# Early expert products as three products of rounded parts, and the key picks laid out by place

## The reference

```
q  = (t @ w_q).reshape(n_tok, 8, 2, 128)               # 256 tokens, 1024 -> 2048
sc = einsum("thpd,hpnd->thpn", q, subkeys)             # scores of 128 keys, two halves
sv, si = top_k(sc, 16)                                 # 16 best keys of each half
cand = sv[:, :, 0, :, None] + sv[:, :, 1, None, :]     # 16 x 16 sums
cidx = si[:, :, 0, :, None] * 128 + si[:, :, 1, None, :]
top_v, pos = top_k(cand, 16)
idx = take_along_axis(cidx, pos);  g = softmax(top_v)  # 8 x 16 = 128 experts of 16384 a token
h = einsum("cd,ced->ce", x, u_tab[idx])
out = einsum("ce,ced->cd", g * gelu(h), v_tab[idx])
```

## Time and profile before

| | |
|---|---|
| median of 3 runs | 2599.25 us (2597.35 to 2600.2) |
| profiled execution, its own time | 2601.88 us |
| its span in the profile | 2600.1 us |
| granted TensorE clock, mean | 0.99 |
| busy share TensorE (matmuls), VectorE, ScalarE, GpSimd | 97%, 76%, 50%, 29% |
| HBM read | 420.11 MB, 163 GB/s over the span |
| share of the chain that ended last: TensorE, VectorE, ScalarE | 84%, 8%, 3% |
| first expert layer, its early products and batches | 824.0 to 1007.0 us |

### The profile page before, as it was taken

How to read it: one execution, slowest core, us unless ns; L and a number is a source line. 1 busy time by engine, 2 the same in 40 slices (tenths; PEclk the granted TensorE clock), 3 DMA queues, 4 the chain that set the end, 5 groups by cost and what they waited for, 6 DMA issues and landing times.

```text
span 2600.1 us, 44298 instructions
## 1 busy us (share of the span) xinstructions
PE 2517.9 (97%) x14328; PEld 2216.0 (85%) x14328; DVE 1973.4 (76%) x3589; ACT 1288.8 (50%) x1917; POOL 745.1 (29%) x754
## 2 busy tenths in 40 slices
PE   8799998999999999999999999899999999999998
PEld 6689877998889898888888888789898888888887
DVE  6868768786678998577777777679997577777776
ACT  4756557664552265444444444662265444444443
POOL 0400003000000101255555555320101255555554
PEclk9999999999999999999999999999999999999999
...
DMA packets 170081, 424.66 MB, mean 163 GB/s; under 512 B 13517, under 2 KB 66125, under 8 KB 169214
## 3 DMA queue, kind: packets, MB, share of 16 engines
...
...
HBM read 420.11 MB, written 3.18 MB: 163 GB/s over the span
## 4 chain that ended last, share of the span: by engine, by line
PE 84%; DVE 8%; ACT 3%; issue 3%; DMA 1%; DVEq 1%; POOL 1%; ACTq 0%; POOLq 0%; SPq 0%
PE PS L467 16%; PE PS L468 16%; PE PS L469 16%; PE PS L753 13%; PE PS L842 7%; PE PS L755 7%; DVE oh L2278 2%; PE PS L868 2%; PE PS L481 2%; PE PS L482 2%; PE PS L486 2%; DVE oh L2275 1%; DVE lo L1560 1%; PE PS L662 1%; PE PS L810 1%
## 5 line engine op out<-in xcount | busy, mean ns | idle before, releaser
L1560 DVE TENSOR_TENSOR lo<-raw,hi 128x1024 fp32r<-128x1024 f32 x716 | 1060.3, 1507 | 477.6 <-ACT hi L1010 476.3
L1010 ACT ACTIVATE hi<-raw 128x1024 fp32r<-128x1024 f32 x716 | 747.2, 1052 | 298.8 <-PE PS L469 232.3
L467 PE MATMUL PS<-hi,Ah 128*128 128x512 f32 x1024 | 402.0, 393 | 5.1 <-POOL Al L2445 2.6
L468 PE MATMUL PS<-lo,Ah 128*128 128x512 f32 x1024 | 401.1, 392 | 0.0
L469 PE MATMUL PS<-hi,Al 128*128 128x512 f32 x1024 | 398.9, 390 | 0.0
L753 PE MATMUL PS<-xx,hi 128*128 128x512 f32 x1504 | 371.6, 390 | 0.0
L753 PEld LDWEIGHTS PS<-xx,hi 128*128 128x128 f32 x1504 | 282.5, 188 | 58.4
L1465 ACT ACTIVATE gl<-gl 128x256 f32<-128x256 f32 x188 | 78.5, 417 | 479.8 <-DVE gl L2321 479.8
L2445 POOL TENSOR_TENSOR Al<-kept,Ah 128x256 fp32r<-128x256 f32 x188 | 299.8, 1595 | 14.8
L467 PE MATMUL PS<-xx,hi 128*128 128x256 f32 x992 | 281.6, 284 | 0.0
L469 PE MATMUL PS<-xx,lo 128*128 128x256 f32 x992 | 281.3, 284 | 0.0
...
## 6 DMA issues: line engine op xcount, KB each, us to landing
raw<-in_peer_u SPq DMA_DIRECT2D x256, 512.0 KB, 3.6
raw<-in_peer_v SPq DMA_DIRECT2D x256, 512.0 KB, 4.4
...
```

The costliest lines, as they stand in the source:

```text
L467: pe.matmul(o, ah, bh, start=start, stop=False)
L468: pe.matmul(o, ah, bl, start=False, stop=False)
L1010: cp.activation(hi[:, s, 0:size], raw[:, s, 0:size], ACT.Copy).then_inc(hi_made, 1)
L1560: V.tensor_tensor(lo[:, s, 0:size], raw[:, s, 0:size], hi[:, s, 0:size].bitcast(F32), ALU.subtract).then_inc(lo_made, 1)
```

## The change

In the expert layers, with the names of the diff:

- **More early products, most of them in three parts.** LEAD is 38, 24 of them ahead of the transposes. The first THREE = 25 are computed as `hi` by `xh`, `hi` by `xl` and `lo` by `xh`, in order: 16 matmuls, a wait for the low part, 8 matmuls. The high part is ScalarE's (`u_high`, into four places of the arena, `lead_his`), the low part GpSimd's (`u_low`, into `lo`). SyncE waits for `u_low` instead of `split_used` before it loads such a slot again. The last 13 stay in full precision, so the four additions of `xw` come after product 24 of the three-part kind.
- **Order on GpSimd.** 20 `u_low`, the picks, 5 `u_low`, the additions of `xw`.
- **Picks by place.** The table's outermost axis is m, so a pick writes 256 neighbouring columns. The reduction over m becomes four additions of halves (2048, 1024, 512 and 256 columns a partition). VectorE's part of the weights moves between the two halves' picks. GpSimd's compares get a second operation, times 1.0.
- **Batches.** VectorE first copies first keys and every fourth second key into `firsts`, five to a batch, and compares five groups of 128 in one instruction; three scaled compares follow. The fourth token's one-hot is scaled by its weight on ScalarE (`scaled_to`, two batches ahead). TensorE's operands move accordingly. VectorE waits before batch HOTS - 1 until product THREE - 1 has been computed.
- **First values.** VectorE weighs 16 rows in groups of four, where it did so with 12; ScalarE's first four splits of v wait for h0 + 4p + 8. GpSimd's first two `lead_low` wait for four weighed rows.
- **Places.** Four early rows lie in `spare` (over the places of `Ah` and `Al`), the next 16 in `early`.
- **Attention.** GpSimd's doubling and its addition get a second operation with a constant (plus 0.0; times 1.0 first).

```diff
@@ -98,9 +98,11 @@
-LEAD = 34
-LEAD_FIRST = 20
-LEAD_AFTER = (-1, 3, 8, 14, 19, 24, 30, 35, 40, 46, 51, 57, 63, 63)
+LEAD = 38
+LEAD_FIRST = 24
+THREE = LEAD_FIRST + 1
+LEAD_AFTER = (-1, 6, 11, 15, 20, 25, 30, 35, 40, 46, 51, 57, 63, 63)
+PICK_AT = 20
@@ -152,6 +154,8 @@
+    lead_lows = {plan[f"peer{l}"][0] + j: THREE * l + j + 1 for l in range(2) for j in range(THREE)}
@@ -192,6 +196,7 @@
+        spare = sb("spare", [P, 4, T], F32, offset=here[0])
@@ -201,10 +206,11 @@
-        kept = sb("kept", [P, KEPT - IN_X - 16, T])
+        kept = sb("kept", [P, KEPT - IN_X - 20, T])
...
+        lead_his = [sb(f"lead_hi{n}", [P, 2, BLK], F32R, offset=arena_at + 4 * word) for n, word in enumerate((12288, 29184))]
@@ -226,20 +232,31 @@
+        firsts = con[:, C_MASK:C_MASK + 5 * T // 4].rearrange("p (b t) -> p b t", t=5)
         def bank(n):
...
         def lead_row(layer, j):
-            if j < 16:
-                s = (plan[f"peer{layer}"][0] + LEAD + j // 4) % RING
+            if j < 4:
+                return spare[:, j, :]
+            if j < 20:
+                s = (plan[f"peer{layer}"][0] + LEAD + j // 4 - 1) % RING
...
-                return kept[:, j - 16, :]
+                return kept[:, j - 20, :]
...
+        def lead_hi(j):
+            return lead_his[j % 4 // 2][:, j % 2, :]
+        def lead_lo(j):
+            return lo[:, (j + RING - THREE) % RING, :]
@@ -394,7 +411,7 @@
-        seltmp = [view(8192, TT * PH, TOPK, TOPK), view(4096, TT * PH, TOPK, TOPK)]
+        seltmp = [view(8192, TOPK, TT * PH, TOPK), view(4096, TOPK, TT * PH, TOPK)]
@@ -825,7 +842,10 @@
-                    pe.wait_ge(raw_in[s], landed[n])
+                    if j < THREE:
+                        pe.wait_ge(S("u_high"), THREE * layer + j + 1)
+                    else:
+                        pe.wait_ge(raw_in[s], landed[n])
@@ -836,8 +856,19 @@
+                    if j < THREE:
+                        for k in range(KD):
+                            w = lead_hi(j)[:, k * P:(k + 1) * P]
+                            pe.matmul(PS[:, bk, 0:T], w, xh[:, k, :], start=k == 0, stop=False)
+                            pe.matmul(PS[:, bk, 0:T], w, xl[:, k, :], start=False, stop=False)
+                        pe.wait_ge(S("u_low"), THREE * layer + j + 1)
+                        for k in range(KD):
+                            m = pe.matmul(PS[:, bk, 0:T], lead_lo(j)[:, k * P:(k + 1) * P], xh[:, k, :],
+                                          start=False, stop=k == KD - 1)
+                        m.then_inc(split_used, 1)
+                        return
...
-                        if j == 0 and k % 2 == 0:
+                        if j == THREE and k % 2 == 0:
@@ -863,10 +894,13 @@
-                    pe.wait_ge(S("hot_made"), 5 * (64 * layer + b + 1))
+                    pe.wait_ge(S("hot_made"), 4 * (64 * layer + b + 1))
...
-                        i = pe.matmul(PS[:, bk, k * P:(k + 1) * P], oh[:, b % HOTS, 0, k * P:(k + 1) * P],
-                                      oh[:, b % HOTS, 1, k * P:(k + 1) * P], start=True, stop=True)
+                        if k == 3:
+                            pe.wait_ge(S("hot_scaled"), 64 * layer + b + 1)
+                        x = (k + 1) % 4 * P
+                        i = pe.matmul(PS[:, bk, k * P:(k + 1) * P], oh[:, b % HOTS, 1, x:x + P],
+                                      oh[:, b % HOTS, 0, k * P:(k + 1) * P], start=True, stop=True)
@@ -1414,7 +1448,19 @@
+                def u_high(j):
+                    n = u_block(layer, j)
+                    act.wait_ge(raw_in[n % RING], landed[n])
+                    if j >= 4:
+                        act.wait_ge(split_used, u_block(layer, j - 4) + 1)
+                    cp.activation(lead_hi(j), raw[:, n % RING, :], ACT.Copy).then_inc(S("u_high"), 1)
+                u_high(0)
...
+                for j in range(1, 4):
+                    u_high(j)
@@ -1424,16 +1470,20 @@
-                for j in range(10):
-                    lead(j)
+                def leads_to(first, end):
+                    for j in range(first, end):
+                        lead(j)
+                        if j + 4 < THREE:
+                            u_high(j + 4)
+                leads_to(0, 14)
...
-                for j in range(10, LEAD_FIRST - 2):
-                    lead(j)
+                leads_to(14, LEAD_FIRST - 3)
...
-                for j in range(LEAD_FIRST - 2, LEAD_FIRST):
-                    lead(j)
+                leads_to(LEAD_FIRST - 3, LEAD_FIRST)
@@ -1443,12 +1493,25 @@
+                at = [0]
+                def scaled_to(n):
+                    while at[0] < min(n, 64):
+                        b = at[0]
+                        act.wait_ge(S("hot_made"), 4 * (64 * layer + b) + 1)
+                        o = oh[:, b % HOTS, 1, 0:P]
+                        cp.activation(o, o, ACT.Copy, scale=selT[:, 2, 4 * b + 3:4 * b + 4]).then_inc(S("hot_scaled"), 1)
+                        at[0] += 1
...
+                        scaled_to(b + 2)
...
+                            scaled_to(b + 4)
@@ -1475,7 +1538,7 @@
-                    act.wait_ge(S("lead_weighed"), h0 + 4 * p + 4)
+                    act.wait_ge(S("lead_weighed"), h0 + 4 * p + 8)
@@ -2238,16 +2301,20 @@
-                    last([V.scalar_tensor_tensor(seltmp[c][:, :, :, m], rows, float(m), keys[:, :, m:m + 1].to_broadcast([P, TT * PH, TOPK]),
+                    st = seltmp[c]
+                    last([V.scalar_tensor_tensor(st[:, m], rows, float(m), keys[:, :, m:m + 1].to_broadcast([P, TT * PH, TOPK]),
...
-                    V.tensor_reduce(sel[:, c].rearrange("p t k -> p (t k)"), seltmp[c].rearrange("p g k m -> p (g k) m"),
-                                    AX.X, ALU.add).then_inc(S("sel_made"), 1)
+                    for n in (8, 4, 2):
+                        link(V.tensor_tensor(st[:, 0:n], st[:, 0:n], st[:, n:2 * n], ALU.add))
+                    V.tensor_tensor(sel[:, c].rearrange("p t k -> p (t k)"), st[:, 0].rearrange("p g k -> p (g k)"),
+                                    st[:, 1].rearrange("p g k -> p (g k)"), ALU.add).then_inc(S("sel_made"), 1)
...
-                dve.wait_ge(S("weights_tanh"), layer + 1)
-                link(V.tensor_scalar(tv, tv, -1.0, 1.0, ALU.mult, ALU.add))
-                V.reciprocal(tv, tv).then_inc(S("weights_recip"), 1)
+                    if not c:
+                        dve.wait_ge(S("weights_tanh"), layer + 1)
+                        link(V.tensor_scalar(tv, tv, -1.0, 1.0, ALU.mult, ALU.add))
+                        V.reciprocal(tv, tv).then_inc(S("weights_recip"), 1)
@@ -2257,12 +2324,14 @@
-                    w = (2 - m) * T
-                    dst = selT[:, 2 * m:2 + m, :].rearrange("p a b -> p (a b)")
-                    V.tensor_copy(dst, PS[:, 4 + (n - 1) % 4, 0:w]).then_inc(S("sel_turned"), 1)
+                    bk = 4 + (n - 1) % 4
+                    if m == 0:
+                        V.tensor_copy(firsts[:, :, 0:4], PS[:, bk, T:2 * T].rearrange("p (b t) -> p b t", t=4))
+                        V.tensor_copy(firsts[:, :, 4], PS[:, bk, 0:T].rearrange("p (b t) -> p b t", t=4)[:, :, 3])
+                    V.tensor_copy(selT[:, 2 * m, :], PS[:, bk, 0:T]).then_inc(S("sel_turned"), 1)
...
-                iota4 = iota.unsqueeze(1).to_broadcast([P, 4, P])
+                iota5 = iota.unsqueeze(1).to_broadcast([P, 5, P])
@@ -2270,15 +2339,18 @@
-                    first = oh[:, b % HOTS, 1, :].rearrange("p (t i) -> p t i", t=4)
-                    chosen = selT[:, 1, bass.ds(4 * b + 4 * ex, 4)].unsqueeze(2).to_broadcast([P, 4, P])
-                    V.tensor_tensor(first, iota4, chosen, ALU.is_equal).then_inc(hot, 1)
-                    for k in range(4):
+                    first = oh[:, b % HOTS].rearrange("p c x -> p (c x)")[:, 0:5 * P].rearrange("p (t i) -> p t i", t=5)
+                    chosen = (firsts[:, bass.ds(b + ex, 1), :].rearrange("p b t -> p (b t)").unsqueeze(2)
+                              .to_broadcast([P, 5, P]))
+                    V.tensor_tensor(first, iota5, chosen, ALU.is_equal).then_inc(hot, 1)
+                    for k in range(3):
...
-                        V.tensor_scalar(oh[:, b % HOTS, 0, k * P:(k + 1) * P], iota, selT[:, 0, bass.ds(t, 1)],
+                        V.tensor_scalar(oh[:, b % HOTS, 1, (k + 1) * P:(k + 2) * P], iota, selT[:, 0, bass.ds(t, 1)],
...
+                    if b == HOTS - 1:
+                        dve.wait_ge(split_used, u_block(layer, THREE - 1) + 1)
@@ -2304,16 +2376,16 @@
-                for p in (1, 2):
+                for p in (1, 2, 3):
...
-                for p in range(3, LEAD - 13):
-                    weigh_lead(p + 13)
+                for p in range(4, LEAD - 16):
+                    weigh_lead(p + 16)
...
-                    split(M + LEAD - 13 + n)
+                    split(M + LEAD - 16 + n)
@@ -2321,7 +2393,7 @@
-                for p in range(LEAD - 9, LEAD + 3):
```

(34 more changed lines are left out.)

10 lines of the change are left out of this document (removed).

## The result

The changed kernel takes 2638.99 us (median of 4, 2637.61 to 2658.5) against 2598.32 us before (median of 4): a ratio of 1.0174, 95% interval 1.0138 to 1.021. It is **41 us slower**; 2590 was predicted, with a range of 2576 to 2616.

A forecast was written before the change was run, and what follows sets the result against it. TensorE, busy 97% of the span, was taken as the bound, tied with VectorE in the batches. Per layer +7.0 − 1.5 + 2.6 − 11.0 = −2.9; two layers −6, attention −3: 2599.25 − 9 = 2590 us, range 2576 to 2616.

The forecast's parts named there:

- The step that failed: Routing: each GpSimd block subtraction of 1024 columns holds VectorE 1.3 us, between bounds of 0.53 and 2.1.
- full-hold rival: Routing: hold grows with columns to 2.1 us, 10 meetings, joint +17.7, 2612 us in all; chance 0.33.
- 8 such meetings: Routing: VectorE meets GpSimd's two-input work 8 times: candidates one, index arithmetic one, pick product one, blocks five; 1.3 us each.
- The joint: Where TensorE's early products and VectorE's routing meet before the batches: 900.6 instead of 893.5, +7.0 us per layer.
- GpSimd's own chain: Low parts queued behind key picks make TensorE reach the joint at about 896 instead of 893, covered by VectorE's 900.6.
- The batches: Batch stretch after the joint: VectorE's batch 1.52 us instead of 1.63, stretch 112.0 against 113.5, −1.5 us per layer.
- The four sums: GpSimd's sums rebuilding the whole input, moved behind product 24: about 1 us for meetings with VectorE in the batches.
- rival that ScalarE's scaled copy becomes the bound: Batches: TensorE's fourth matmul waits 0.1 us in each batch, +6 us per layer, 2603 us; chance 0.09.
- The first values: First value blocks after the batches: rounds of 3.8 us against TensorE's 2.75, +2.6 us per layer, bounds 0 and 4.
- The main loop: Expert main loop: four experts lose their hidden product there, 4 × 2.76 = −11.0 us per layer.
- Attention: GpSimd's doubling and addition with a second operation: 3 us gained in all, bounds 8 gained and 2 lost.
- Picks by place: VectorE's routing: contiguous picks at 5.4 and 3.4 us instead of 8.0 and 4.6, reduces 4.7; chain saves 3.3 us.

The follow-up runs named there:

- e5: Changed kernel without early products in three parts: 34 in full precision, 20 ahead of the transposes, GpSimd's sums before its picks; 2616.41 us, 1.007 of the kernel before.
- e2: Changed kernel with all 16 second-key picks on VectorE and none on GpSimd; 2644.21 us, 1.0178 of the kernel before.
- e9: Changed kernel with 14 three-part products, sums ahead of the picks, low parts 8 and later waiting for VectorE's candidate additions; 2606.05 us, 1.0031 of before.
- e1: Kernel before with only the attention edit, GpSimd's doubling and addition given two operations each; 2597.67 us, 1.0002 of the kernel before.
- e10: e9 plus 12 rows weighed before the first split, ScalarE's third rounding before its fourth split, a VectorE wait for GpSimd's low parts; 2587.68 us, 0.9961 of before.

## Why the prediction was wrong

- **The step that failed:** "A one-input instruction of 256 columns held 0.16, two inputs of 1024 are eight times that: 1.3 us. I take 1.3." A meeting with a subtraction holds VectorE until that subtraction ends: 10.95 − 2.60 over four additions is 2.09 each. The prediction's upper bound, 2.1, was the value. The 0.16 that it scaled was read beside GpSimd's compares, and these are the one kind of GpSimd's work in the routing that does not hold whole (0.2 of 1.13 us). The full-hold rival had the mechanism. It is the rule of the Trainium skill (SBUF — State Buffer, section "SBUF: two separate sides"); the trace agrees with it for GpSimd's subtractions, sums and pick product, and not for its compares. The rival's 2612 was too small as well: its joint, +17.7, was near, but it took over the forecasts for the batches and the first values.
- **The count failed with it.** "I count 8 such meetings: one at the candidates". There are four instructions at the candidates and four meetings, since each one queues behind a new subtraction. In the whole routing of the first layer 12 of VectorE's instructions are held by subtractions or by the pick product: four at the candidates, two in the index arithmetic, three in the first tree with its last addition, one at 892.52 and two of the second picks. The full-hold rival counted 10. From the conversion to the transposes' copies VectorE takes 72.7 us in the changed kernel (835.89 to 908.63) and 51.4 in e5 (841.29 to 892.67). The 21.3 are 8.35 at the candidates, 4.2 in the index arithmetic (9.23 against 4.99), 4.1 in the tree (11.51 against 7.44), 2.1 at the one-input instruction at 892.52 and 2.7 in the second picks. MAX8 and the reciprocal, for which the forecast counted nothing, were free; one-input arithmetic was not (2.44 and 2.35 us).
- **The joint** was put at +7.0 and measured +20.9. The forecast for GpSimd's own chain, that it would make TensorE wait (to 896) and be covered by VectorE, was right in kind: TensorE waited 12 us for low part 20, and e2 shows that this cost nothing at the transposes.
- **The batches** were put at −1.5 and came at +5.1 and +6.1. The form itself gives −1.0 (e5). The four sums, costed at 1 us, hold VectorE some 4 us (913.6 to 919.2) just when TensorE has no spare batch: it waits 2.5 and 1.3 us. The clock is at the lower level for a while behind each pause, and no term stood for that. In e9, where the sums stand ahead of the picks and no long pause precedes the batches, the stretch is 112.7. The rival that ScalarE's scaled copy becomes the bound did not come: e5 has that copy too, and its stretch is shorter than before's.
- **The first values** were put at +2.6, between 0 and 4, and came at +6.0 and +6.7. The rounds took 3.7 us, and 3.8 was forecast. Not seen was what is queued behind them on ScalarE: the third rounding, so that TensorE's third value waits 5.0 us and starts at the lower clock.
- **The main loop**, −11.0 net, was exact. **Attention**, put at −3, is 0: GpSimd's additions did become more than twice as fast (1.17 to 0.51 us), but the time did not change (e1).
- **Picks by place** were to save 3.3 us, which is part of the sum for the joint, and save nothing. 16 picks fall from 8.01 to 6.45, not to 5.4, since the compares delay some of them. The first tree with its last addition takes 7.4 us beside GpSimd's product (e5), where the reduce took 4.42 beside the same product: with one input it was not held. Both halves together take 22.1 us (e5) where they took 21.5.

The premise, six products for the price of five, holds for TensorE's own time (2.88 us each in e9), and e10 comes to 2588 with 14 of them. What was mis-sized was the price of making low parts on GpSimd beside VectorE.
